# One core, four network layers: the order of side work in two projection groups, and one gate tile moved ahead of the attention mixing

## The reference, cut to what matters

```
h    = rms_norm(x, norm1_w)
proj = h @ w_in            # q 1024, kv 6*256, nsa gates 24, dn qkv 3072, z 1024, a 8, b 8, merge gates 4096
# sparse attention: compressed, selected and window branches
k_c  = rope(kv[0]);  v_c = kv[1]
kc   = gelu(blocks(k_c + pe) @ w1_k) @ w2_k       # 15 blocks of 32 tokens, stride 16
vc   = gelu(blocks(v_c + pe) @ w1_v) @ w2_v
p    = masked_softmax(q @ kc);   o_cmp = p @ vc   # then selected and window attention
o_nsa = g0 * o_cmp + g1 * o_sel + g2 * o_win
# delta net: convolution over 4 tokens, silu, l2norm of q and k, chunks of 64 tokens
qkv  = silu(conv(dn_qkv));  q, k = l2norm(q), l2norm(k)
tinv = inverse(1 + lower(kb @ k.T * decay));  state recurrence over 4 chunks
mixed = sigmoid(g_nsa) * (o_nsa @ w_up_nsa) + sigmoid(g_dn) * (o_dn @ w_up_dn)
x    = x + mixed @ w_o;   x = x + ffn(rms_norm(x))
```

## Time and profile before

| | us |
|---|---|
| median of 3 runs | 2346.88 |
| lowest, highest | 2345.47, 2350.53 |
| the profiled execution's own time | 2346.51 |
| span of the trace in it | 2344.7 |
| PE busy | 2302.2 (98%) |
| DVE busy | 1468.6 (63%) |
| ACT busy | 1298.4 (55%) |
| mean granted clock of PE | 0.996 |

### The profile page before, as it was taken

The page is one execution under the profiler, slowest core; times in us unless marked ns, Lnnn a source line. Parts: engine busy times, 40 slices in busy tenths (PEclk is TensorE's granted clock), DMA queues, the critical chain, the costliest instruction groups (busy, mean ns, idle before and its releaser), DMA issues.

```text
span 2344.7 us, 32560 instructions
## 1 busy us (share of the span) xinstructions
PE 2302.2 (98%) x12152; PEld 1941.0 (83%) x12152; DVE 1468.6 (63%) x2548; ACT 1298.4 (55%) x2374; POOL 18.4 (1%) x38
## 2 busy tenths in 40 slices
PE   8999999999999999999999999999999999999998
PEld 7877888788888888867888888888888888888886
DVE  4554565665665666867777666756566566665554
ACT  5644555666555545755556546546555555554444
POOL 1000000000000000000000000000000000000000
PEclk9999999999999999999999999999999999999999
DMA  7555566565445555665453326555666666665554
GB/s 230 166 166 148 172 202 197 152 183 170 134 142 191 154 180 179 186 191 168 137 169 115 102 81 234 198 187 178 190 189 189 189 189 189 189 207 191 192 190 164
DMA packets 232429, 409.09 MB, mean 174 GB/s; under 512 B 21505, under 2 KB 46385, under 8 KB 231889
## 3 DMA queue, kind: packets, MB, share of 16 engines
q1 hardware_dynamic: 228256, 393.07, 54.1%
q0 software_dynamic: 3152, 10.59, 1.2%
q10 hardware_dynamic: 864, 3.35, 0.4%
HBM read 400.66 MB, written 6.29 MB: 174 GB/s over the span
## 4 chain that ended last, share of the span: by engine, by line
PE 92%; ACT 3%; DVE 3%; DMA 1%; issue 1%; ACTq 0%; DVEq 0%; POOL 0%; SPq 0%; POOLq 0%
PE banks L410 51%; PE banks L374 17%; PE banks L376 8%; PE banks L404 5%; PE banks L848 1%; PE banks L688 1%; ACT weights_high L342 1%; DVE weights_low L345 1%; PE banks L2389 1%; PE banks L2400 1%; PE banks L859 0%; DMA weight_ring<-in_w_in 0%; PE banks L1214 0%; PE banks L867 0%; PE banks L868 0%
## 5 line engine op out<-in xcount | busy, mean ns | idle before, releaser
L345 DVE TENSOR_TENSOR weights_low<-weight_ring,weights_high 128x512 fp32r<-128x512 f32 x1464 | 998.1, 691 | 781.0 <-ACT weights_high L342 750.3
L342 ACT CAST weights_high<-weight_ring 128x512 fp32r<-128x512 f32 (+2 forms) x1476 | 904.6, 619 | 962.4 <-PE banks L410 597.4
L410 PE MATMUL banks<-weights_high,hidden_T 128*128 128x512 f32 x2976 | 857.4, 400 | 6.8 <-DVE weights_low L345 5.2
L410 PEld LDWEIGHTS banks<-weights_high,hidden_T 128*128 128x128 f32 x2976 | 549.3, 189 | 128.0 <-issue 11.6
L374 PE MATMUL banks<-hidden_T,weights_high 128*128 128x512 f32 x1728 | 543.3, 396 | 1.3 <-DVE weights_low L345 0.8
L410 PE MATMUL banks<-weights_low,hidden_T 128*128 128x512 f32 x1488 | 461.4, 391 | 0.0
L376 PEld LDWEIGHTS banks<-hidden_T,weights_low 128*128 128x128 f32 x1728 | 324.6, 188 | 76.7
L376 PE MATMUL banks<-hidden_T,weights_low 128*128 128x256 f32 x1728 | 339.5, 278 | 0.0
L410 PEld LDWEIGHTS banks<-weights_low,hidden_T 128*128 128x128 f32 x1488 | 280.0, 188 | 61.1
L374 PEld LDWEIGHTS banks<-hidden_T,weights_high 128*128 128x128 f32 x1728 | 263.1, 189 | 2.3 <-DVE weights_low L345 1.5
L410 PE MATMUL banks<-weights_high,ffn_high 128*128 128x512 f32 x344 | 106.3, 390 | 1.6 <-DVE weights_low L345 1.6
(11 more groups left out here) (427 smaller groups left out, 1793.8 us busy)
## 6 DMA issues: line engine op xcount, KB each, us to landing
weight_ring<-in_w_in SPq DMA_DIRECT2D x168, 512.0 KB, 3.5
weight_ring<-in_w_gla_in SPq DMA_DIRECT2D x96, 512.0 KB, 3.8
weight_ring<-in_w_gate SPq DMA_DIRECT2D x88, 512.0 KB, 3.9
weight_ring<-in_w_ffn_up SPq DMA_DIRECT2D x88, 512.0 KB, 3.8
weight_ring<-in_w_down SPq DMA_DIRECT2D x88, 512.0 KB, 3.7
weight_ring<-in_w_mla_in SPq DMA_DIRECT2D x48, 512.0 KB, 3.7
weight_ring<-in_w_gla_out SPq DMA_DIRECT2D x32, 512.0 KB, 4.4
weight_ring<-in_w_mla_out SPq DMA_DIRECT2D x32, 512.0 KB, 4.3
```

Source lines behind the costliest of these rows:

```text
L342: nc.scalar.copy(hi, raw).then_inc(high_ready, 1)
L345: nc.vector.tensor_tensor(lo, raw, hi.bitcast(F32), ALU.subtract).then_inc(low_ready, 1)
L410: last = pe.matmul(ps[:, b + t, 0:width], a[:, t * P:(t + 1) * P], w, start=(k == 0 and n_th == 0), stop=(k == kt - 1 and n_th == 2))
```

## The change

Four parts, all of them order; no operation is added or taken away.

A. The last chunk of the first group is evicted without its two row scalings. They become `scale_raw` and run in slots 4 and 10 of the second group.

B. Second group. The key blocks are added two a slot (slots 60 and 61), the value blocks in slots 63, 64, 66 and 67, and the query rotations follow. The logarithms move from slots 70, 71, 72, 77, 78, 79 of this group and 2, 3 of the next to slots 72, 74, 75, 79 and 0, 1, 3, 4 of the next, with the logarithm of the decays at 77 instead of 75. The last three sums on PE move by one tile.

C. Third group. The steps from the fold to the scores move one tile later on PE, and DVE's steps with them; the turn of KS moves from p = 26 to p = 16, that of KW from p = 28 to p = 24. The centring of the scores moves from slots 21 and 22 to slots 22 and 23, the sums from slot 26 to 27, the probabilities from 27 to 28, the exponential on ACT from 24 to 25. The turn of the probabilities stays at p = 30.

D. PE multiplies one gate tile (`one()`) ahead of its wait for the turned probabilities. From there on, each gate tile stands one place earlier among PE's other work; the splits on ACT and DVE keep their places.

```diff
@@ nsa_input_tensor
-                elif 76 <= p < 79:
-                    prepare_sum(pe, p - 73)
+                elif 77 <= p < 80:
+                    prepare_sum(pe, p - 74)
...
-                elif p == 26:
+                elif p == 16:
                     prod_n.wait_chunk(pe, 4)
                     pe.wait_ge(n_rot, 3)
                     pe.wait_ge(ab_cexp, 1)
                     turn_n.tensor(pe, KS)
-                elif p == 28:
+                elif p == 24:
                     pe.wait_ge(c_centred, 1)
                     turn_n.tensor(pe, KW)
@@ nsa_tensor
+            one()
             turn_cp.wait(pe)
             turn_n.wait(pe, KW)
@@ the scalar side work of the second group
-            for g in range(3):
-                yield from pace.to(70 + g)
+            for g, slot in enumerate((72, 74, 75)):
+                yield from pace.to(slot)
                 root_logarithm(g)
@@ the vector side work of the second group
+        def scale_raw(n, f):
+            V(nc.vector.tensor_tensor(dn_raw(n, f), dn_raw(n, f), over(joint2.row.unsqueeze(1), [P, 2, S]), ALU.mult))
...
+                if f in (1, 3):
+                    scale_raw(dn_apart, f // 2)
...
                     yield from pace.to(60)
                     turn_n.wait(v, KC)
                     next(key_blocks)
+                    next(key_blocks)
                     yield from pace.to(61)
-                    next(key_blocks)
+                    for _ in key_blocks:
+                        pass
@@ the vector side work of the third group
-            yield from pace.to(21)
+            yield from pace.to(22)
             v.wait_ge(c_scored, 1)
...
-                yield from pace.to(22)
+                yield from pace.to(23)
             v.sem_inc(c_centred, 1)
-            yield from pace.to(26)
+            yield from pace.to(27)
             v.wait_ge(c_exped, 1)
...
-            yield from pace.to(27)
+            yield from pace.to(28)
@@ to_raw
-                for f in range(2):
-                    V(v.tensor_tensor(dn_raw(n, f), dn_raw(n, f), row, ALU.mult))
+                if n < dn_apart:
+                    for f in range(2):
+                        scale_raw(n, f)
```

110 lines of the change are left out of this document (56 added, 54 removed).

## The result

| | before | after |
|---|---|---|
| median of 5 runs | 2346.24 us | 2354.34 us |
| lowest, highest | 2344.80, 2350.53 | 2352.53, 2355.92 |
| profiled execution, its span | 2346.51, 2344.7 | 2355.92, 2354.1 |
| PE busy | 2302.2 | 2307.7 |
| ratio after/before, 95% interval | | 1.0035 (1.0023 to 1.0046) |

What follows compares the result with a forecast made beforehand. TensorE (PE), busy 2302.2 of 2344.7 us, was taken as the bound. Terms -1.5 - 4.3 + 6.4 + 6.2 = +6.8 on the profiled 2346.51 gave 2353.3 us; range 2349.0 to 2357.5.

Steps and rivals of the forecast that it cites:

- A: Start of the second group: PE's wait of 1.68 us shrinks as two row scalings go behind splits; -1.5 us.
- B: Second group's compress blocks: a wait of 2.44 and its clock fall go, less late weights; -4.3 us.
- the late tile 70: Second group, after the first compress block: weights cast 5.95 us after issue, so PE waits 0.9 us.
- the waits of 0.42 and 1.01 shrink too: Second group: waits for late weights and for a split behind a logarithm and its table load shrink.
- C: Third group: waits at the turn of KW (+3.2) and L607 (+1.4), and a clock fall (+1.7); +6.4 us.
- The chain: Third group, turn of KW: DVE's head, centrings and split end 3.2 us after PE ends tile 23; +3.2 us.
- D: Gate tile ahead of the mixing: later splits in the DeltaNet stage cost 3.6 and 3.3, 0.7 gained; +6.2 us.
- a clock fall that I had as a rival: DeltaNet stage: clock also falls after the waits of 2.5; 2355.0 us, chance 0.14 shared with the later-ring rival.
- The two big waits: DeltaNet stage, behind the second L2382 in each batch of heads: PE waits 2.5 us for a low split.
- The small ones: DeltaNet stage, two earlier places per batch: late splits cost 0.5 and 0.5, then nearly 0.2 and 0.5 us.
- D's saved tile: End of the DeltaNet stage: one gate tile less is left; between 0 and -1.36, taken as -0.7 us.
- The clock: Half-clock falls: one removed at the first compress block (1.71 us), one added at the turn of KW (+1.7).

Runs made afterwards that it cites:

- a_alone: The kernel before with only the last chunk's two row scalings moved behind splits of the second group; median 2344.25 us, ratio 0.9990.
- no_tile_ahead: The changed kernel without the gate tile ahead of the mixing, the other three parts kept; median 2350.06 us, ratio 1.0017 to the kernel before.
- a_and_b_alone: The changed kernel with the third group's functions of before (logarithms 4 to 7 in slots 0 to 3) and without `one()`; median 2342.30 us, ratio 0.9985 to before.

## Why the prediction was right, and where its terms were off

The direction, the places and, by the medians, the size were right: +6.8 forecast, +8.1 measured (5.4 to 10.8 by the interval). The profiled stretch has +6.2, or +4.7 with the seam's 1.45 counted. Point by point:

- **A**, -1.5: right. The wait went from 1.68 to 0.23, and a_alone shows that the scalings cost nothing in their slots.
- **B**, -4.3: too much by 1.2. Measured -3.1. The latency was right (5.90 against 5.95), and so was the late tile 70 (0.63 in place of 0.9). The step that failed is "the waits of 0.42 and 1.01 shrink too", put at 1.43 with 0.4 for what follows tile 70. In their place stand 0.53, 0.40 and 0.48 at tiles 72, 73 and 75. In the changed kernel each of these three splits starts behind rotation operations on DVE, 0.3, 0.7 and 2.1 after its cast has ended. In the eleven profiled executions with two key blocks a slot the wait at tile 70 is the time from the issue of its weights to their cast less 5.28: 0.18 at 5.45, 0.63 at 5.91, 0.84 at 6.12. By the estimate from the rule of the Trainium skill (DMA: Bandwidth & Descriptors, section "Anatomy of one DMA — SWDGE (gpsimd) path"), 4.4 us for the two transfers, tile 70 would not have waited; it does in all eleven.
- **C**, +6.4: measured +5.4 in the profile, which has no clock fall there; without its 1.7 for the clock the forecast is +4.7. The chain was 0.6 longer than worked out, 3.77 for 3.2: the split of tile 26 starts 0.3 before PE ends tile 23, not 0.6, since the head before it is in its way, and the gaps between the steps make up the rest. L607 was 1.36 for 1.4. The clock fall did not come in this execution, but it came in the two others that have the wait.
- **D**, +6.2: measured +3.9, of which 1.7 is a clock fall that I had as a rival; without it +2.2, so this is the term that was furthest off. The addends as written come to 3.5 and 3.2, not 3.6 and 3.3, which is 0.2 of it. The two big waits are 2.44 and 2.35 for 2.5 each. The small ones, by how much further the starts on PE are behind after each place, are 0.2 and 0.5 in the first batch and 0.2 and 0.6 in the second, 1.5 for 1.7 in all. The step that failed is that I let almost nothing be made up. The stage did have idle time to give back: 0.7 ahead of L2367, where PE waited 0.69 for ACT, and some 1.0 in the two batches, 0.36 of it the wait at L2402.
- **D's saved tile**, -0.7 in this sum: too little. It was put at half a tile because of the chain through the loads. It brings 1.60, its 1.36 and 0.2 of smaller steps, in each of the six kernels with the tile ahead, late or not. The loads are issued that much earlier too: PE has 9.0 to 9.4 us to go to the waiting tile in these six and 8.9 to 9.8 in the other eight. The further 0.46 at that tile (0.40 for 0.86) is within what the loads vary by.
- The tile of the earlier trace rows is not the up projection's first, as the earlier trace rows and the prediction call it, but its thirteenth (252 tiles lie between it and the start of the second group, 240 of them of the three groups).
- **The clock**: the term was zero in sum (one fall removed, one added), and so it is in the two traces, but by luck: the fall added came in the DeltaNet stage and not at KW. The mean of the runs has +1.8 to +2.5 (depending on which of the means before is taken, with an error of 0.6), with the falls ahead of the change in it. What of this the change brings is not shown.

Without the clock the terms were -1.5, -2.6, +4.7 and +6.2, and the trace has -1.45, -1.4, +5.4 and +2.2: D was too high by 4.0, and B and C took 1.9 of that back. That the sum of 6.8 lies nearer to the medians' 8.1 than the 4.7 found place by place is luck too. The rest, free of the clock by its count, has grown by 5.6 to 5.8, with an error of 0.8, which is within reach of the 4.7; the traces show no place for more.

Do the parts add? A and B -3.9 by the medians, C +7.8 (no_tile_ahead less a_and_b_alone), D +4.3 (after less no_tile_ahead): the whole 8.1 but for rounding, by construction. C by place is +5.4 in the trace of the changed kernel and +7.0 in that of no_tile_ahead, with its clock fall. D by itself on the kernel before was +5.6. With the uncertainty of the ratios, some 2 us, they agree.

What stays open: why the clock falls behind one wait and not behind its equal, below; what makes tile 70's weights take from 5.45 to 6.12 us and the loaded gates from 5.8 to 8.0 from execution to execution; and whether the tile ahead is a gain once a split is moved for it.

## What to carry to other kernels

Before an instruction is moved ahead on one engine, write down where the chain that it waits for begins. If the chain's first step waits for the moved engine's own progress, moving it only turns cover into a wait: here three places of 1.36 each decided whether 3.77 us were seen. A tile put into a wait is saved at the end of the filler work (1.60 here, and 0.7 of idle time on the way), but every later tile then stands one place earlier against its split, and where the splits come late that is paid: 5.2 us in the two batches, 1.6 once a split was moved. The better edit was to take the copy ahead of a split it had no need to follow, which took 1.32 off the wait and moved no tile.

## What the runs showed of the hardware that I had not expected

The clock's fall is not decided by the length of the wait. In this region of the program nine profiled executions had, in all, 15 waits of PE of 2.0 to 3.8 us. Behind seven of them the granted clock was 0.50 (1.2 GHz) for 3.41 us, behind eight it stayed at 1.00. The wait of 3.77 has two falls in three executions, that of 2.44 at the first compress block two in three, the first wait of 2.4 in the DeltaNet stage two in four, the second, of 2.35, none in four, and the one of 2.04 inside the up projection one in one. No wait of 1.8 us or less in this region had a fall behind it. So in these executions a wait of this size cost its length and, about every second time, 1.7 us more.

A transfer of 512 KB on SyncE's queue, issued right behind another of 512 KB, was cast 5.45 to 6.12 us after its issue in the fourteen profiled executions (tile 70's weights), while the core moved 188 GB/s in the trace of before and 225 in that of after.
